# A hybrid decoder layer on 8 cores: x and y transposed, k, v and q begun while x arrives, GLU, attention and a 4-shift-packed convolution in one phase, output projection in halves

## The chip, the cores and the metric

One Trainium2 chip, 8 of its cores, each running the same program on its own share of the data. The metric is the device time of one execution in microseconds (us), taken on the slowest core. Engines: PE is TensorE (matmuls), PEld its weight loads, DVE is VectorE, ACT is ScalarE, POOL is GpSimd, SP issues DMAs.

## The reference: what is computed

One layer with two parallel groups behind one input projection, for a prompt (4 sequences of 2048) and for 32 single decode rows; model width 2048.

```python
h = rms_norm(x, norm_mix_g)
z = h @ w_in                      # columns: q 1024 | k 256 | v 256 | u_val 1024 | u_gate 1024
q = rope(rms_norm(q, q_norm_g), pos); k = rope(rms_norm(k, k_norm_g), pos)
a = attn(q, k, v, sinks)          # 16 heads of 64, 4 kv heads, window 128, a sink logit per head
u = u_val * sigmoid(u_gate)       # GLU
c = causal_dwconv(u, 31 taps); c = silu(layer_norm(c))
x = x + concat(a, c) @ w_out
x = x + square(relu(rms_norm(x, norm_mlp_g) @ w_up)) @ w_down   # 2048 -> 8192 -> 2048
```

Outputs are y, the new k, v and convolution states of the prompt, and those of the decode rows.

## The kernel before

Each core has 1024 prompt columns (half a sequence), the 128 rows before them (the halo, needed for keys and for the convolution) and 4 decode rows. Activations lie transposed, channels on the 128 partitions and tokens along the free axis: HT is the normed x in bf16 (16 channel tiles of 1160 columns), XT the residual in f32 (16 tiles of 1032: 1024 prompt, 4 decode, 4 padding), HM the input of the MLP. A weight tile is 128x128, and a projection is 16 matmuls over the input channels for each piece of columns.

The program is a list in the order of the Python code; a planner (`P.add`) gives every operation to its engine in that order and adds semaphore waits from the buffers read and written. So each engine works in order, and the order of the code is the order of its stream. Helpers record all operations of one kind, so these lines stand for many: L490 is every matmul, L494 every transpose on PE, L458 every activation on ScalarE, L462 every two-input operation of VectorE or GpSimd, L476 and L477 copies and casts (ScalarE, and VectorE or GpSimd), L445 every DMA except those of wq (L573). "arena" in the profile is the one SBUF buffer that everything lies in, "psum" the eight PSUM banks.

The stages, one after another:

1. **x** (to 64.0 us). SP loads ten row tiles of x; ScalarE makes the sums of squares (L546), VectorE scales (L551), and PE transposes each tile twice: in f32 for XT (304 transposes in all) and in bf16 for HT. GpSimd makes the rope tables, issues wkv (4 DMAs), and then wq (16) when the last x tile is in.
2. **k/v** (to 102.4) and **q** (to 168.2). Ten tiles of k/v, then nine of q, each followed by `qk_chain`, which takes norm and rope from PSUM on ScalarE, VectorE and GpSimd. `fin_qk` transposes the result.
3. **GLU** (to 288.6). For 8 channel chunks a gate and a value projection, each over three banks (`acc3`, two slots of three banks in turn, pieces of 356 columns), a sigmoid and a product. VectorE runs the 31 taps of convolution chunks 0 and 1 as multiply-adds (`conv_tap`, L718) beside it.
4. **Convolution** of chunks 2 to 7 on PE (288.6 to about 370): 31 matmuls with a diagonal matrix for each of three pieces; GpSimd builds the diagonals (multiplies of 3968 columns). Then the LayerNorm sums by matmul, until 386.6.
5. **Attention** (386.6 to 456.2). 16 units (block of 128 queries, pair of kv heads), `unit_a` and `unit_b`: 4 score matmuls and 4 that add the mask, 4 exponentials of 512 columns, 8 matmuls for output and denominator with 64 output partitions each, then 1/x as Ln and Exp. GpSimd normalizes the convolution (`ln_chunk_a`, L841) beside it. Decode attention follows, to 469.7.
6. **Output projection** (469.7 to 607.7): 16 chunks of 48 matmuls over AT (attention) and CT (convolution). After each, VectorE adds the residual, and `norm2_stats` squares the chunk before (one in four on VectorE) and adds it up by two matmuls of 512 columns.
7. **MLP** (to 1557.8): 16 groups of four hidden tiles. `up_group` is issued one group ahead of `down_group`. In the last group `out_chunk` transposes each y chunk back in f32 (nine transposes on PE, three copies on ScalarE) and stores it.

## Time and profile before

| | us |
|---|---|
| median of 6 runs (1560.15 to 1561.43) | 1560.88 |
| the profiled execution, its own time | 1559.33 |
| its span on core 5, the slowest (others from 1551.2) | 1557.8 |
| PE busy in it, matmuls and transposes | 1457.0 (94%) |
| DVE, ACT, POOL busy | 725.6, 294.1, 260.9 |
| DMA moved | 113.83 MB, 73 GB/s in the mean |
| PE's share of the chain that ended last | 87% |

The span is cut out of one execution on one core. Busy times overlap, since engines work beside each other. In a row of the timeline the first number is when it starts and the second how long it lasts, then engine, line, operation, output<-input, how many instructions it holds, and in brackets how long the engine was idle before and what ended that. In a row of the table by lines and form there stand count, busy time, mean ns of one, and idle time before. Matmuls are pipelined, so the mean of one can be longer than the step from one to the next.

### The profile page before, as it was taken

To read this page: it belongs to the slowest core of one execution; us is meant where nothing else is said; L and a number is where in the kernel's file an instruction comes from. 1 tells how busy PE (TensorE), PEld (TensorE's weight loads), DVE (VectorE), ACT (ScalarE), POOL (GpSimd) and SP (SyncE) were. 2 spreads that over 40 slices of the span, in tenths; PEclk is the share of its full clock that TensorE was granted. 3 is DMA by queue.
4 is the path that set the end of the run, shared out by engine and by line. 5 is a ranking of instruction groups with operands and counts; after the bars stand their busy time and mean duration, and the time that the engine had idled before them with its cause. 6 is when DMAs were issued, how large, how long until landed. Compare 5 with 4: busy or idle time off the path is not lost.

```text
span 1557.8 us, 23496 instructions; the slowest of 8 cores (1551.2 to 1557.8 us)
## 1 busy us (share of the span) xinstructions
PE 1457.0 (94%) x9650; PEld 926.0 (59%) x9650; DVE 725.6 (47%) x686; ACT 294.1 (19%) x456; POOL 260.9 (17%) x276
## 2 busy tenths in 40 slices
PE   3799999998979899999999999999999999999997
PEld 3444566664226556666666666666666666666665
DVE  5534268895233211263454454364355345355353
ACT  5633200102773212101001000000100100100113
POOL 2346302353920000101001000000100100100000
PEclk9999999999889999999999999999999999999999
DMA  9830244002005342746146246245335435425315
GB/s 235 181 61 36 41 76 74 17 2 15 1 10 86 56 75 47 122 82 106 31 82 108 38 73 109 47 68 103 56 67 95 67 56 95 75 54 89 68 58 161
DMA packets 63009, 113.83 MB, mean 73 GB/s; under 512 B 18882, under 2 KB 38658, under 8 KB 61724
## 3 DMA queue, kind: packets, MB, share of 16 engines
q0 software_dynamic: 43744, 90.77, 35.6%
q1 hardware_dynamic: 19160, 21.56, 4.4%
q8 instruction: 78, 1.28, 0.3%
q14 instruction: 27, 0.22, 0.1%
HBM read 194.12 MB, written 10.35 MB: 131 GB/s over the span
## 4 chain that ended last, share of the span: by engine, by line
PE 87%; DVE 4%; ACT 3%; issue 3%; DMA 3%; ACTq 0%; DVEq 0%; SPq 0%; POOL 0%; POOLq 0%
PE psum L490 85%; DVE arena L462 3%; PE psum L494 2%; ACT arena L458 1%; ACT arena L476 1%; DMA arena<-wup 1%; DMA arena<-xm 1%; DVE arena L477 1%; DMA arena<-wo 0%; DMA arena<-tab 0%; DVE arena L551 0%; ACT arena L546 0%; ACTq L255 0%; DVEq L255 0%; SPq L445 0%
## 5 line engine op out<-in xcount | busy, mean ns | idle before, releaser
L490 PE MATMUL psum<-arena 128*128 128x344 bf16 (+5 forms) x9086 | 1405.5, 317 | 49.5 <-DVE arena L462 30.5
L490 PEld LDWEIGHTS psum<-arena 128*128 128x128 bf16 (+3 forms) x9086 | 875.2, 98 | 568.2 <-issue 113.2
L462 DVE TENSOR_TENSOR arena<-psum,arena 128x1032 f32<-128x1032 f32 (+10 forms) x400 | 418.5, 1064 | 359.9 <-PE psum L490 268.0
L462 DVE TENSOR_TENSOR arena<-arena 128x1032 bf16<-128x1032 bf16 (+3 forms) x144 | 141.8, 987 | 375.2 <-ACT arena L458 368.2
L458 ACT ACTIVATE arena<-psum 128x1032 bf16<-128x1032 f32 (+8 forms) x160 | 128.0, 803 | 928.8 <-PE psum L490 904.4
L445 POOL DMA_DIRECT2D arena<-wup x64 | 33.9, 531 | 804.6 <-PE psum L490 804.6
L462 POOL TENSOR_TENSOR arena<-arena 128x256 f32<-128x256 f32 (+6 forms) x64 | 138.8, 2171 | 141.1 <-PE psum L490 63.6
L718 DVE SCALAR_TENSOR_TENSOR arena<-arena 128x1032 f32<-128x1032 bf16 (+1 forms) x90 | 123.3, 1370 | 9.4 <-DVE arena L718 0.5
L458 ACT ACTIVATE arena<-arena 128x1032 bf16<-128x1032 f32 (+10 forms) x139 | 80.7, 590 | 133.5 <-DVE arena L462 98.9
L494 PE MATMUL psum<-arena 128*128 128x128 f32 (+6 forms) x564 | 61.5, 255 | 47.3 <-DVE arena L551 27.8
L494 PEld LDWEIGHTS psum<-arena 128*128 128x128 f32 (+6 forms) x564 | 52.1, 125 | 59.3 <-issue 54.5
L476 ACT COPY arena<-psum 128x512 f32<-128x512 f32 (+9 forms) x115 | 54.3, 514 | 84.3 <-PE psum L494 74.9
L483 DVE TENSOR_REDUCE arena<-arena 128x4 f32<-128x256 bf16 (+4 forms) x20 | 16.3, 817 | 64.9 <-ACT arena L458 64.8
L445 POOL DMA_DIRECT2D arena<-wdn x64 | 34.0, 551 | 2.8 <-issue 2.6
L445 POOL DMA_DIRECT2D arena<-wo x16 | 8.6, 540 | 129.7 <-PE psum L490 129.7
L445 POOL DMA_DIRECT2D arena<-wu x16 | 8.7, 543 | 74.7 <-PE psum L490 74.7
L458 ACT ACTIVATE arena<-psum,arena 128x1032 f32<-128x1032 f32 (+2 forms) x7 | 6.8, 978 | 73.3 <-PE psum L490 73.3
L546 ACT ACTIVATE arena<-arena 128x2048 bf16<-128x2048 f32 (+1 forms) x10 | 19.2, 1922 | 6.5 <-DVE arena L487 5.3
L573 POOL DMA_DIRECT2D arena<-wq x16 | 10.6, 701 | 34.6 <-DMA arena<-xs 34.6
L551 DVE TENSOR_SCALAR arena<-arena 128x2048 bf16<-128x2048 f32 (+1 forms) x10 | 12.8, 1281 | 4.7 <-ACT arena L458 4.4
L477 DVE CAST arena<-arena 128x1032 bf16<-128x1032 f32 (+1 forms) x12 | 11.8, 1027 | 0.8 <-PE psum L490 0.7
L841 POOL TENSOR_SCALAR arena<-arena 128x1032 f32<-128x1032 f32 x8 | 9.6, 1201 | 1.4 <-POOL arena L462 1.4
(17 smaller groups left out, 35.8 us busy)
## 6 DMA issues: line engine op xcount, KB each, us to landing
arena<-wup POOLq DMA_DIRECT2D x64, 512.0 KB, 6.9
arena<-wdn POOLq DMA_DIRECT2D x64, 512.0 KB, 14.1
arena<-xm SPq DMA_DIRECT2D x8, 1024.0 KB, 10.3
arena<-wu POOLq DMA_DIRECT2D x16, 512.0 KB, 6.2
arena<-wo POOLq DMA_DIRECT2D x16, 512.0 KB, 6.2
yp<-arena SPq DMA_DIRECT2D x16, 512.0 KB, 3.2
arena<-wq POOLq DMA_DIRECT2D x16, 256.0 KB, 14.4
arena<-wkv POOLq DMA_DIRECT2D x4, 512.0 KB, 20.4
```

The costliest lines, as they stand in the source:

```text
L445: return P.add(eng, lambda e: e.dma_start(out=out.ap, in_=in_.ap), reads=[in_], writes=[out], key=key, group=group, final=final)
L458: return P.add("act", lambda e: e.activation(out=out.ap, in_=in_.ap, func=func, bias=b, scale=s), reads=rd, writes=[out])
L462: return P.add(eng, lambda e: e.tensor_tensor(out=out.ap, in0=in0.ap, in1=in1.ap, op=op), reads=[in0, in1], writes=[out])
L476: return P.add("act", lambda e: e.copy(out=out.ap, in_=in_.ap), reads=[in_], writes=[out])
L477: return P.add(eng, lambda e: e.tensor_copy(out=out.ap, in_=in_.ap), reads=[in_], writes=[out])
L483: return P.add("dve", lambda e: e.tensor_reduce(out=out.ap, in_=in_.ap, axis=AX.X, op=ALU.add), reads=[in_], writes=[out])
L490: return P.add("pe", lambda e: e.matmul(out.ap, lhsT.ap, rhs.ap, start=start, stop=stop), reads=[lhsT, rhs], writes=[out])
L494: return P.add("pe", lambda e: e.transpose(out.ap, in_.ap, ident.ap), reads=[in_, ident], writes=[out])
L546: P.add("act", (lambda xn=xn, xin=xin, ms=ms, pp=pp: (lambda e: e.activation(out=xn(p=pp).ap, in_=xin(p=pp).ap, func=AF.Square, accum_out= ...
L551: P.add("dve", (lambda xn=xn, xin=xin, rs=rs, pp=pp: (lambda e: e.tensor_scalar(out=xn(p=pp).ap, in0=xin(p=pp).ap, scalar1=rs.ap, scalar2= ...
L573: P.add("pool", (lambda kc=kc: (lambda e: e.dma_start(out=WQ(kc).ap, in_=wq_d[kc])))(), writes=[WQ(kc)], key="wq", group=True, after=xin_d ...
L718: P.add("dve", (lambda c=c, uu=uu, cc=cc, j=j: (lambda e: e.scalar_tensor_tensor(out=cc.ap, in0=uu.ap, scalar=CW(c).ap[:, j:j + 1], in1=cc.ap,
```

## The change

Nearly all of the program's first half is written anew (1468 lines of diff); the MLP's matmuls and loads stay. What it does:

- **Start.** The host hands x over transposed; 16 channel tiles of 1160 columns arrive through SP. As each lands, VectorE scales it by the norm's gain into HT, ScalarE squares it, GpSimd adds the squares, and PE multiplies three (later more) k/v tiles by it. The row scale is applied after the projections. GpSimd issues a wkv tile between the sums and wq after the last. K's `qk_chain` reads the projection from an SBUF copy (RAW). q follows in nine tiles.
- **One phase for GLU, attention and convolution.** For a channel chunk there are six `u_job` (3 pieces of 352, 352 and 356 columns, gate and value) on two PSUM banks, 6 and 7. The sigmoid is made of Exp, Ln, Exp on ScalarE, with a product on VectorE before and one on GpSimd after. Between the jobs stand two attention units a chunk, and from the third chunk on two `conv_job`. The mask is a product on VectorE in place of a matmul; decode attention (`sample_a`, `sample_b`) stands in chunk 4.
- **Convolution in 32-partition strips.** `u_done` copies u by 16 DMAs from SBUF to SBUF into U4, in four shifts and four groups of 32 channels. A matmul then takes four taps at once for 32 channels; a `conv_job` is 8 steps of 4 such strips, 512 columns wide, in all 512 matmuls. VectorE makes no taps. `conv_sums` adds up for LayerNorm on GpSimd.
- **Output projection.** First the AT half for all 16 chunks (`wo_half(dc, 0, AT)`), beside it the LayerNorm; then the CT half with the residual and `norm2`. x is loaded a second time for the residual. Squares are added on GpSimd (14 of 16), not by matmuls.
- **MLP.** Three wup tiles are loaded ahead, not two. The last down group stores XT as it is, transposed; the host turns it back.

```diff
-        for h8 in range(2):
-            pt = ps_bf16(nbank(), (8, 128))
-            for j in range(8):
-                c = 8 * h8 + j
-                tr(pt(j, (0, nt)), xn((c * 128, c * 128 + 128), p=pp), IDB((0, nt), p=(0, nt)))
-            tt("dve", HT((8 * h8, 8 * h8 + 8), (c0, c0 + nt)), pt((0, 8), (0, nt)),
-               bc(PAR((8 * h8, 8 * h8 + 8)), 2, (128, 8, nt)), ALU.mult)
+    for kc in range(16):
+        xs_ = XST[kc % 4]
+        xd.append(dma("sp", xs_(), R(xt_d[kc]), "xst%d" % (kc % 4)))
+        dma("pool", WKV(kc), R(wkv_d[kc]), "wkv%d" % kc, after=[xd[kc - 3]] if kc >= 3 else [])
+        if kc == 5:
+            dma("sp", PAR(), R(par_d), "par")
+            dma("sp", CST(), R(cst_d), "cst")
+        if kc == 8:
+            dma("sp", TABIN(), R(tab_d.rearrange("p (a b c) -> p a b c", a=2, b=10)), "tab")
+        ts("dve", HT(kc), xs_(), G1(kc), ALU.mult)
+        if kc == 0:
+            act(SS1(), xs_(), AF.Square)
+        else:
+            act(SQX[kc % 2](), xs_(), AF.Square)
+        if kc >= 2:
+            tt("pool", SS1(), SS1(), SQX[(kc - 1) % 2](), ALU.add)
+        for ti in range(NKV1):
+            tn, c0, nt = TT[ti]
+            mm(kvp[ti](p=(0, nt)), HT(kc, (c0, c0 + nt)), WKV(kc), kc == 0, kc == 15)
+    tt("pool", SS1(), SS1(), SQX[1](), ALU.add)
+    for kc in range(16):
+        dma("pool", WQ(kc), R(wq_d[kc]), "wq%d" % kc, after=[xd[15]] if kc >= 2 else [xd[13]])
...
-        qk_chain(acck, 4, nt, GCK, GSK, ti, kb_, kout(p=pp), out_f32=kf4)
+        qk_chain(RAW[ti], 4, nt, GCK, GSK, ti, kb_, K2[ti](p=pp), out_f32=kf)
...
+    for kc in range(16):
+        for i in range(3):
+            q_mm(1 + i, i, kc)
+    fin_k([0, 1, 2, 3], 6)
+    fin_k([4, 5, 6, 7], 7)
+    fin_k([8, 9], 6)
+    pend = [q_chain(1, 0), q_chain(2, 1)]
+    for i, ti in enumerate(range(4, 10)):
+        for kc in range(16):
+            q_mm(ti, i % 3, kc)
+        if i == 0:
+            pend.append(q_chain(3, 2))
+        fin_q(*pend.pop(0))
+        pend.append(q_chain(ti, i % 3))
...
-            if j == 0:
-                act(SG(), accb((0, 3), (0, UW)), AF.Sigmoid)
-                if dve_taps:
-                    conv_tap(*dve_taps.pop(0))
+    def u_job(c, pi, w, gate):
+        a, b = PU[pi]
+        n = b - a
+        acc = dense_bank(n)
+        for kc in range(16):
+            mm(acc(), w(kc), HT(kc, (U0 + a, U0 + b)), kc == 0, kc == 15)
+        flush()
+        i = gts[0] % 2
+        if gate:
+            gt, sg = GT[i]((0, n)), SGR[i]((0, n))
+            rb = RB((a, b))
+            tt("dve", gt, acc(), rb, ALU.mult)
+            act(gt, gt, AF.Exp, scale=-1.0)
+            act(gt, gt, AF.Ln, bias=1.0)
+            act(gt, gt, AF.Exp, scale=-1.0)
+            tt("pool", sg, gt, rb, ALU.mult)
+        else:
+            sg = SGR[i]((0, n))
+            tt("dve", UB[c % 2]((a, b)), acc(), sg, ALU.mult)
+            if pi == 2:
+                tt("dve", UF(c), acc((322, 356)), SGR[i]((322, 356)), ALU.mult)
+            gts[0] += 1
...
+    def u_done(c):
+        ub, u4 = UB[c % 2], U4[c % 2]
+        first = None
+        for s in range(4):
+            for g in range(4):
+                src = Ref(ub.ap[32 * g:32 * g + 32, 2 + s:2 + s + UL], ub((0, NU)).rngs)
+                dst = Ref(u4.ap[32 * s:32 * s + 32, g, 0:UL])
+                i = 4 * s + g
+                P.add("sp", (lambda src=src, dst=dst: (lambda e: e.dma_start(out=dst.ap, in_=src.ap)))(),
+                      reads=[src], writes=[u4()] if i == 0 else [], claim=[u4()] if i == 15 else [],
+                      key="u4%d" % (c % 2))
...
-        for pi, (a, b) in enumerate(PM):
-            a0 = 172 if (c == 2 and pi == 0) else a
-            n_ = b - a0
-            for j in range(31):
-                g0 = MC0 + a0 + j - 30
-                mm(accb(pi, (0, n_)), dg(j), U(c, (g0, g0 + n_)), j == 0, j == 30)
+    def conv_job(c, pi):
+        acc = dense_bank(512)
+        for t in range(8):
+            for g in range(4):
+                mm(acc(p=(32 * g, 32 * g + 32)), D4[c % 2](g, t),
+                   U4[c % 2](g, (4 * t + 512 * pi, 4 * t + 512 * pi + 512)), t == 0, t == 7)
+        flush()
+        act(CC(c, (512 * pi, 512 * pi + 512)), acc(), AF.Identity, bias=CB(c))
+    def conv_sums(c, eng="pool"):
+        act(SQT(), CC(c), AF.Square)
+        if c == 0:
+            cp(eng, S1(), CC(c))
+            cp(eng, S2(), SQT())
+        else:
+            tt(eng, S1(), S1(), CC(c), ALU.add)
+            tt(eng, S2(), S2(), SQT(), ALU.add)
...
-                mm(pss(), IDB(), bc(mb(), 1, (128, 4, 128)), False, True)
+                act(pt(), ps_f32(2 * kb + gi, 1, (4, 128))(), AF.Exp, scale=0.125)
+                tt("dve", pt(), pt(), bc(mb(), 1, (128, 4, 128)), ALU.mult)
...
+    for c in range(8):
+        wg, wv = wu.pop(0), wu.pop(0)
+        for pi in range(3):
+            for gate in (True, False):
+                u_job(c, pi, wg if gate else wv, gate)
+                if c == 0 and pi == 0 and gate:
+                    while pend:
+                        fin_q(*pend.pop(0))
+                if job % 3 == 1 and nu < 16:
+                    if nu >= 1:
+                        unit_b(nu - 1)
+                    unit_a(nu)
+                    nu += 1
+                if c == 4 and pi == 0 and not gate:
+                    sample_a()
+                if c == 4 and pi == 1 and not gate:
+                    sample_b()
+                job += 1
+            if c >= 2 and pi < 2:
+                conv_job(c - 2, pi)
+                if pi == 1:
+                    conv_sums(c - 2)
+        u_done(c)
...
-        if dc >= 1:
-            norm2_stats(dc - 1)
-            act(HM(dc - 1), XT(dc - 1), AF.Identity, scale=G2(dc - 1))
+    conv_job(6, 0)
+    conv_job(6, 1)
+    conv_sums(6, "dve")
+    unit_b(15)
+    conv_job(7, 0)
+    conv_job(7, 1)
+    conv_sums(7, "dve")
+    xt_load(7)
+    xt_load(8)
+    wo_half(0, 0, AT)
+    wo_half(1, 0, AT)
+    wo_half(2, 0, AT)
+    ln_stats()
+    for dc in range(3, 16):
+        wo_half(dc, 0, AT)
+        if dc - 3 < 8:
+            ln_chunk(dc - 3)
+    def norm2(dc):
+        sq = SQ2[dc % 2]
+        act(HM(dc), XT(dc), AF.Identity, scale=G2(dc))
+        act(sq(), XT(dc), AF.Square)
+        if dc == 0:
+            cp("pool", SS(), sq())
+        else:
+            tt("pool" if dc < 14 else "dve", SS(), SS(), sq(), ALU.add)
+    for dc in range(16):
+        wo_half(dc, 1, CT)
+        norm2(dc)
+    upq = [wstream(wup_d[i], "wup", 128) for i in range(3)]
...
-            if last and dc >= 1:
-                out_chunk(dc - 1)
+            if last:
+                dma("sp", R(yt[128 * dc:128 * dc + 128, :]), XT(dc, (0, NO)), "yt%d" % dc, final=True)
```

In the order of each engine's stream, at three places:

On PE, the end of the GLU, the convolution and the start of attention before (356 columns is a GLU piece, 34x128, 128x120 and the pieces of 172 and 344 are state, decode and prompt convolution with LayerNorm sums, 512 columns attention):

```order
L490 MATMUL psum<-arena 128x356 x720
L494 MATMUL psum<-arena 34x128 x8
L490 MATMUL psum<-arena 128x172 x31
L490 MATMUL psum<-arena 128x344 x62
L494 MATMUL psum<-arena 128x120 x8
L490 MATMUL psum<-arena 128x344 x513
L490 MATMUL psum<-arena 128x512 x8
L490 MATMUL psum<-arena 64x512 x8
```

and one channel chunk of the new phase (352 and 356 columns is GLU, 64x512 and 128x512 attention, 32x512 the convolution's strips):

```order
L483 MATMUL psum<-arena 128x356 x16
L483 MATMUL psum<-arena 128x352 x32
L483 MATMUL psum<-arena 64x512 x8
L483 MATMUL psum<-arena 128x512 x4
L483 MATMUL psum<-arena 32x512 x32
L483 MATMUL psum<-arena 128x352 x32
L483 MATMUL psum<-arena 32x512 x32
L483 MATMUL psum<-arena 128x356 x16
L483 MATMUL psum<-arena 64x512 x8
L483 MATMUL psum<-arena 128x512 x4
```

GLU, convolution and attention were three blocks; now no more than 32 matmuls of one kind stand in a row.

On POOL, the start before (640 columns are the rope tables, 256 the K chains):

```order
L462 TENSOR_TENSOR arena<-arena 128x640 x4
L487 MEMSET arena 128x16x4
L487 MEMSET arena 128x256
L487 MEMSET arena 128x16x4 x2
L445 DMA arena<-wkv 128x4x512 x4
L573 DMA arena<-wq 128x1024 x16
L462 TENSOR_TENSOR arena<-arena 128x256 x2
L477 CAST arena<-arena 128x256
```

and now, from the last of the sums of squares (1160 columns) on:

```order
L437 DMA arena<-wkv 128x512
L454 TENSOR_TENSOR arena<-arena 128x1160 x2
L437 DMA arena<-wq 128x1024 x16
L473 CAST arena<-arena 128x128 x4
L473 CAST arena<-arena 128x32
L454 TENSOR_TENSOR arena<-arena 128x640 x4
L480 MEMSET arena 128x8x4
L454 TENSOR_TENSOR arena<-arena 128x256 x2
L473 CAST arena<-arena 128x256
```

The wq issues stand behind fifteen sums of squares, and the tables and the five casts between them and the first K chain.

On PE, the last down group before (each y chunk's transposes behind the next chunk's 12 matmuls):

```order
L490 MATMUL psum<-arena 128x344 x5976
L494 MATMUL psum<-arena 128x128 x8
L494 MATMUL psum<-arena 4x128
L490 MATMUL psum<-arena 128x344 x12
L494 MATMUL psum<-arena 128x128 x8
L494 MATMUL psum<-arena 4x128
```

and now, from the last GLU job to the end:

```order
L483 MATMUL psum<-arena 128x356 x16
L483 MATMUL psum<-arena 32x512 x64
L483 MATMUL psum<-arena 64x512 x8
L483 MATMUL psum<-arena 32x512 x64
L483 MATMUL psum<-arena 128x344 x6921
```

Output projection and MLP are now one run of 6921 matmuls of 344 columns, with no statistics and no transposes among them; four conv jobs and half an attention unit stand before it.

## Rows read from the trace of the kernel before

**Rows 1.** The page: the span, and TensorE's granted clock in 40 slices, in tenths.

```profile
span 1557.8 us, 23496 instructions; the slowest of 8 cores (1551.2 to 1557.8 us)
...
PEclk9999999999889999999999999999999999999999
```

**Rows 2.** Table by stage, core 5 (columns as told above).

```profile
0.00:64.00 64.00, 29.04 (x304) 27.39 (x304) 40.27 (x35) 41.53 (x78) 20.51 (x32) 0.96 0.89 217
386.60:456.20 69.60, 67.76 (x256) 18.77 (x256) 19.43 (x30) 57.83 (x97) 44.92 (x24) 0.90 0.00 1
456.20:469.70 13.50, 2.03 (x57) 1.76 (x57) 4.93 (x8) 7.96 (x13) 1.74 (x3) 0.59 0.34 55
469.70:607.70 138.00, 127.75 (x822) 81.31 (x823) 31.60 (x26) 37.07 (x36) 8.46 (x16) 0.95 0.40 68
668.60:1502.20 833.60, 817.80 (x5592) 544.72 (x5591) 404.35 (x355) 58.78 (x57) 58.25 (x110) 1.00 0.43 73
```

**Rows 3.** Timeline of PE: output projection, second up group, an MLP group, last down group.

```profile
510.07 31.48 PE L490 MATMUL psum<-arena 128*128 128x512 bf16 x200 [2.62 <-DVE arena L462]
...
652.76 16.42 PE L490 MATMUL psum<-arena 128*128 128x344 bf16 x100 [3.10 <-DMA arena<-wup]
...
1359.75 56.20 PE L490 MATMUL psum<-arena 128*128 128x344 bf16 x384 [1.05 <-DVE arena L462]
...
1503.76 1.91 PE L490 MATMUL psum<-arena 128*128 128x344 bf16 x12
...
1507.04 1.91 PE L490 MATMUL psum<-arena 128*128 128x344 bf16 x12
```

**Rows 4.** Table by lines and form, 386.6 to 456.2 us (attention).

```profile
L458 ACT ACTIVATE arena<-psum 128x512 bf16<-128x512 f32 x64 | 37.9, 597 | 9.5 <-PE psum L490 7.7
L462 POOL TENSOR_TENSOR arena<-arena 128x1032 f32<-128x1032 f32 x15 | 35.5, 2366 | 5.6 <-ACT arena L458 4.6
...
L458 ACT ACTIVATE arena<-arena 128x512 f32<-128x512 f32 x30 | 18.8, 626 | 1.4
L462 DVE TENSOR_TENSOR arena<-psum,arena 128x512 f32<-128x512 f32 x15 | 10.2, 682 | 6.8 <-PE psum L490 6.8
```

**Rows 5.** The page: costliest groups, and DMA issues (KB each, us to landing).

```profile
L573 POOL DMA_DIRECT2D arena<-wq x16 | 10.6, 701 | 34.6 <-DMA arena<-xs 34.6
L551 DVE TENSOR_SCALAR arena<-arena 128x2048 bf16<-128x2048 f32 (+1 forms) x10 | 12.8, 1281 | 4.7 <-ACT arena L458 4.4
...
arena<-wup POOLq DMA_DIRECT2D x64, 512.0 KB, 6.9
...
yp<-arena SPq DMA_DIRECT2D x16, 512.0 KB, 3.2
```

**Rows 6.** Timeline of DVE at the start and in the convolution, then of POOL.

```profile
9.06 6.53 DVE L477 CAST arena<-arena 128x128 bf16<-128x128 f32 x4
...
273.88 9.67 DVE L718 SCALAR_TENSOR_TENSOR arena<-arena 128x1032 f32<-128x1032 bf16 x7
...
288.35 12.12 DVE L718 SCALAR_TENSOR_TENSOR arena<-arena 128x1032 f32<-128x1032 bf16 x3
...
282.95 15.03 POOL L462 TENSOR_TENSOR arena<-arena 128x3968 bf16<-128x3968 bf16 x2 [16.74 <-PE psum L490]
```

**Rows 7.** Table by lines and form, whole span: the K chains, a cache load.

```profile
L462 POOL TENSOR_TENSOR arena<-arena 128x256 f32<-128x256 f32 x18 | 12.0, 667 | 22.3 <-DVE arena L462 20.8 <-POOL arena L462 0.6 <-PE psum L490 0.4
...
L445 POOL DMA_DIRECT2D arena<-ck x1 | 4.6, 4620 | 0.0
L462 DVE TENSOR_TENSOR arena<-psum,arena 128x256 f32<-128x256 f32 x9 | 3.7, 415 | 0.0
```

**Rows 8.** Timeline of PE, one q tile.

```profile
145.99 7.07 PE L490 MATMUL psum<-arena 128*128 128x512 bf16 x32
```

**Rows 9.** Table by lines and form, PE, 430.85 to 431.20 us (attention, 64-column matmuls).

```profile
L490 PE MATMUL psum<-arena 128*64 128x512 bf16 x4 | 0.6, 391 | 0.0
```

**Rows 10.** Timeline of SP, four copies between partitions ahead of decode attention.

```profile
385.39 2.49 SPq L445 DMA_DIRECT2D arena<-arena  x4
```

971 lines of the change are left out of this document (417 added, 554 removed).

## The prediction, made before the changed kernel ran

> **What bounds the kernel now.** I read the page first [rows 1]: in a span of 1557.8 us TensorE has its full 2.4 GHz in all but two of 40 slices, so clock is not the matter as a whole. The table by stage [rows 2] says how dense TensorE is where; time can only go where it does work that can be left out, or waits. The MLP from 668.6 to 1502.2 us is dense: 384 matmuls of 344 columns take 56.2 us [rows 3], 146 ns each, in a period of 57.2. Four other places are loose. From 0 to 64 TensorE is busy 29 us, and only with transposes of x. From 288.6 to 386.6 it makes a convolution of 31 taps, and then waits for LayerNorm. From 386.6 to 456.2 (attention) it shows as busy, but ScalarE holds 57.8 of the 69.6 us and a unit's matmuls wait for its exponentials; from 456.2 to 469.7 nearly everything waits. And in the last down group 12 matmuls (1.75 us) are followed by nine f32 transposes and a wait, a pitch of 3.3 us [rows 3].
>
> The profiled execution took 1559.33 us by its own time, 1.5 over its span; the median of the runs is 1560.88. I make the sum in span and add 3.1 at the end.
>
> **Step 1, start to the first GLU matmul: 168.2 us to about 157.** Removed are the 304 transposes of x and their evacuations. In their place x arrives transposed in 16 tiles, and GpSimd adds each tile's squares: 15 adds of 1160 columns, 2.37 us x 1160/1032 = 2.66 each [rows 4]. Between them it issues the wkv loads (0.66 each, as for wq [rows 5]). The row to watch is another: seven multiply-adds on VectorE take 9.7 us while GpSimd is idle, but three take 12.1 us across two GpSimd multiplies that take 15.0 together, and at the start four small casts take 6.5 us beside GpSimd's products [rows 6]. VectorE stands still while a GpSimd instruction runs, if both inputs of its own are in SBUF, or for a plain cast. The scaling of x is of the cast's kind and takes 0.7 us (1.28 for 2048 columns [rows 5], here 1160). So a tile costs 2.66 + 0.66 = 3.3 if nothing excludes, 4.0 if the scaling alternates with all of it; I take 3.7, since it can fall into an issue. First add near 9 us, so the last ends near 64 (58 to 72). x is 9.5 MB, 44 us at the 217 GB/s of now [rows 2], so GpSimd ends last. Only then come, in its order, 16 wq issues (10.6 us [rows 5]), five casts and four table products (about 8 us), and then ten K chains. These now read the projection from SBUF, not PSUM, so they fall under the row above: GpSimd 0.67 twice and a cast of 0.4, VectorE 0.41 and two halves, some 0.55 [rows 7], alternate, about 2.9 us a tile, 29 in all; without exclusion 2.0. K is ready near 112 (103 to 116). TensorE has three kv tiles (10.4 us), some f32 column sums (4 us) and the first three q tiles (96 matmuls at 0.22 us, 21) to do by 101, then waits for K's transposes. Six q tiles of 7.07 us [rows 8] and 0.3 of transposes end at 157 (147 to 168). Gain 11.
>
> **Step 2, GLU, convolution, LayerNorm, both attentions: 301.5 us to about 225.** Removed are 31-tap matmuls for most of eight chunks and all VectorE taps, the mask matmuls and the LayerNorm stall. The GLU's own 768 matmuls stay (0.15 us each by columns, 115). Convolution: 512 matmuls that each write a strip of 32 partitions. No row shows a strip of 32. The nearest row is attention's 64-column matmuls: four take 0.6 us at a mean of 391 ns each [rows 9], so two start together and the next two about 0.22 us later. If four strips start together likewise, 128 groups x 0.22 to 0.24 = 28 to 31 us; if only two, 55; if none, 111. I take 31, since strips that start together is the pattern of the row.
> Per channel chunk TensorE has 6 GLU jobs (14.4 us), two attention units (6 pairs each, 2.8), two conv jobs (3.8), and half a microsecond or so of changes of shape: 21 to 22. ScalarE has nine passes over 352 columns (0.49 each, scaled from 0.63 for 512), eight exponentials at 0.60, four passes at 0.63 [rows 4], two evacuations and a square: 14. VectorE has about 11, GpSimd 9. None exceeds TensorE, but GLU and conv have two banks, 6 and 7, and a bank is free only after gate multiply (0.55), three ScalarE passes, GpSimd's multiply (0.85) and the value multiply (0.55): 4 us with the hand-offs, and one unit's 3.6 us of ScalarE stands in that line twice a chunk, ahead of it. Laying these durations out for one chunk in the order of the streams, TensorE waits 1.2 us at the second gate and 2.6 at the second value: 24.8 us a chunk, 21.4 for the first two, which have no conv. For the exclusion of rows 6 I add 1 us a chunk (0 to 9). At the loop's start TensorE waits 5 us for the last q chain, and GpSimd issues the two cache loads, one of them 4.6 us now [rows 7], ahead of the first gate's multiply: 4 more. 6 x 25.8 + 2 x 22.4 + 9 = 209. The tail: the last chunk's 16 shift copies are issued on SP at up to 0.62 us, as four copies between partitions now [rows 10], so they land 9 to 14 us after the last GLU matmul's evacuation; TensorE covers 7 of that. Tail 16. x comes back as 8.5 MB while the first projection chunks run; its first tile lands just before the first add. 209 + 16 = 225, gain 76.5.
>
> **Step 3, output projection: 138.0 to 129.** Its 768 matmuls (112.3) stay; 32 statistics matmuls (7 us) and four stops of 2.6 us on VectorE's squares [rows 3] go, since squares are now summed on GpSimd (2.4 us against 3.5 of TensorE). Added: f32 LayerNorm sums in two banks with their evacuation (5), VectorE's 3.7 us a chunk against 3.5 (2), and a new wait. The first wup loads stand on GpSimd behind the sum for chunk 13, whose end I put 1 us before the projection's, and land 6.9 us later [rows 5]: 6 plus 2 of slow clock. Without that 121.
>
> **Step 4, MLP up to the last group: 894.5 to 890.** Unchanged but for a stop in the second up group that a third wup load in flight removes: 3.1 us, and the next 100 matmuls take 16.4 [rows 3], 1.8 more than at 146 ns each; I take 4.5. **Step 5, last down group: 55.6 to 34.** 16 x 1.75 = 28.1, then one add (1.2), one issue (0.4, estimated) and 3.2 to 4.5 for the store. Stores go out at 300 GB/s; the backlog is unknown, 0 to 12 us, nearest 0 to 1 since 512 KB lands in 3.2 us now [rows 5].
>
> Sum: -11 - 76.5 - 9 - 4.5 - 21.5 = -122.5, so a span of 1435 and, at the median's 3.1 above span, 1438 us. A measurement of this kernel can tell about 0.2% from no change.
>
> **The rivals.**
> Interleaving hides everything (0.16): TensorE paces the loop, 6 x 22 + 2 x 18 = 168 in place of 209, 1397 us. For it: no engine is above 14 us of 22. Against it: two banks only, and in-order ScalarE.
> VectorE and GpSimd alternate through the loop (0.18): GpSimd reads SBUF for about 9 us a chunk (three gate products, diagonals 1.8, sums 4.7), and eight mask multiplies, now from SBUF, wait in line with the gates. All of it in the chain is 72 us, 8 are counted: 1470 to 1500. Rows 6 speak for it; that VectorE with one PSUM input is 0.68 us with GpSimd at work [rows 4] speaks against it for the gates. The Trainium skill states it as a rule (page "SBUF — State Buffer", section "Who interferes with whom"): two SBUF inputs on VectorE, or one of its two-port fast modes, exclude a GpSimd instruction that reads SBUF, and whoever starts first keeps the port to its end. The trace agrees, with three multiply-adds in 12.1 us. By that rule in full this rival is the forecast.
> The packing does not do what it says (0.10): strips run one after another, +10 us a chunk of which 3.8 falls into waits, and all of it in the tail: some 6 x 6.2 + 20 = 57, about 1495.
> Slower than before (0.03): TensorE at 1.2 GHz. From 456.2 to 469.7, with 2 us of matmuls in 13.5, it is granted 0.59 [rows 2]. Kv, q, GLU, attention and conv are some 265 us of matmuls at full clock. If all ran at half, +265 less 50 of waits they would fill, 1650; it is slower than before when half speed holds for 60% of them. Against it: the loop is planned 85% busy, and 67.8 of 69.6 us in attention kept 0.90.
>
> **How the numbers follow.** Forecast as summed 0.52; the remaining 0.01 is a front end so late that the gain nearly vanishes. 1438 is the forecast's centre; its own range is 1410 to 1465. 1388 takes in the first rival with an early front end, 1497 the second and part of the third. Faster 0.96, same 0.01, slower 0.03.
>
> **What would show it.** Right: the first 352-column matmul at 147 to 168 us; GLU chunks 24 to 27 us apart; four 32-column matmuls starting within 20 ns; a wup wait of about 6 us before the first up group; last matmul 5 to 6 us before the end; period of 57.2 in the MLP unchanged. Wrong: a loop at 22 us a chunk, or at 30 and more with VectorE's mask multiplies far above 0.6 us; strips one by one; stores that land long after the last add; a granted clock near 0.5 in the loop.

## The result, and the profile after

The changed kernel takes **1461.24 us** in the median, against 1561.2 of the kernel before in the same measurement: a ratio of 0.935, with a 95% interval of 0.9338 to 0.9364. That is 100 us less, 6.4%. The forecast was 1438 with a range of 1388 to 1497 and a gain of 122.5; the time lies 23 us above its centre.

One thing is needed to read the numbers: in this kernel pairs of neighbouring cores often have a stretch of some 161 us at a granted clock of 0.81 (from 114 to 276 us here, with a piece at half clock in it), and in the profiled execution cores 6 and 7 have it. Lines of the page, then of the view of the cores:

```profile
span 1459.8 us, 22456 instructions; the slowest of 8 cores (1446.6 to 1459.8 us)
...
PE 1346.1 (92%) x9007; PEld 834.3 (57%) x9016; DVE 696.1 (48%) x734; ACT 286.0 (20%) x424; POOL 312.1 (21%) x330
...
PEclk9988788899899999999999999999999999999999
```

```profile
core 0: 1451.3 us, clock 0.974
...
core 6: 1459.8 us, clock 0.956
```

So I read the stages on core 0, which has no such stretch, and count the 8.5 us to core 6 apart. These 8.5 are a net. Core 6 is 9.6 us later than core 0 at the first GLU matmul, 11.7 at the projection and 15.0 at the last down group (the 3 in the projection come on cores 1 and 5 too, without the stretch); then it gains 6.4, since on core 0 the stores end latest of all eight cores, 16.7 us behind the last matmul for 10.2 on core 6. The profiled execution took 1461.33 by its own time, 1.5 above its span. The table by stage of core 0, cut where the prediction's steps end (a row has its start and end, its length, the busy us and count of PE, of weight loads, of DVE, ACT and POOL, then TensorE's granted clock, the share of the DMA engines, and GB/s); the loop with its tail, and the last down group, answer to [rows 2, 3]:

```profile
0.00:60.70 60.70, 31.65 (x106) 11.14 (x109) 47.73 (x20) 20.01 (x17) 49.85 (x35) 0.92 0.81 214
60.70:153.65 92.95, 82.97 (x430) 39.83 (x435) 52.38 (x79) 38.52 (x91) 72.01 (x77) 0.96 0.54 93
153.65:366.90 213.25, 176.23 (x1412) 93.82 (x1416) 84.45 (x178) 101.52 (x191) 79.05 (x64) 0.94 0.44 74
366.90:391.25 24.35, 11.35 (x138) 4.49 (x137) 8.74 (x15) 5.96 (x10) 3.24 (x3) 0.72 0.79 155
391.25:513.97 122.72, 116.23 (x784) 77.00 (x781) 64.96 (x58) 49.65 (x48) 42.37 (x30) 0.99 0.56 115
513.97:1406.60 892.63, 875.16 (x5960) 582.42 (x5961) 416.67 (x368) 70.03 (x70) 65.67 (x124) 1.00 0.45 75
1406.60:1451.30 44.70, 27.97 (x192) 18.15 (x190) 20.96 (x17) 0.00 (x0) 0.00 (x0) 0.84 0.81 189
```

| step of the prediction | before | forecast | core 0 | off |
|---|---|---|---|---|
| 1: to the first GLU matmul | 168.2 | 157 | 153.65 | -3.4 |
| 2: GLU loop and tail | 301.5 | 209 + 16 | 213.25 + 24.35 | +12.6 |
| 3: output projection | 138.0 | 129 | 122.7 | -6.3 |
| 4: MLP to the last group | 894.5 | 890 | 892.6 | +2.6 |
| 5: last down group | 55.6 | 34 | 44.7 | +10.7 |
| the slowest core's low clock | | 0 | 8.5 | +8.5 |

The sum of the last column, 24.7 (24.8 unrounded), is what the span of 1459.8 has over the forecast's 1435. Step 3 ends where the first up group starts, at 513.97.

The last two channel chunks and the tail on core 0, in the timeline of PE and then of SP:

```profile
345.78 8.40 PE L483 MATMUL psum<-arena 128*128 128x352 bf16 x76 [2.10 <-DVE arena L454]
355.78 12.97 PE L483 MATMUL psum<-arena 128*128 128x352 bf16 x124 [1.59 <-ACT arena L450]
371.29 4.53 PE L483 MATMUL psum<-arena 128*32 128x512 bf16 x40 [2.54 <-DVE arena L454]
386.28 13.89 PE L483 MATMUL psum<-arena 128*32 128x512 bf16 x124 [10.46 <-DMA arena<-arena]
```

```profile
371.17 11.80 SPq L776 DMA_DIRECT2D arena<-arena  x16
...
1409.80 26.58 SPq L437 DMA_DIRECT2D yt<-arena  x16
```

Each chunk has a wait of about 2 us for VectorE and one of 1.6 for ScalarE; the tail one of 10.5 for the copies. The chunks' last GLU matmuls lie 25.2, 25.6, 32.9, 25.9, 25.6 and 25.6 us apart from the third chunk on; 25.8 was forecast, and the 32.9 has decode attention in it.

### The profile page after: what moved, and what is told of

Read it like the earlier page. It is cut to its first block, busy times and chain, and to the rows that moved or that the text cites. A ratio compares the mean times of both kernels' runs of the same rounds, so it can differ in the third digit from the quotient of the medians.

```text
span 1459.8 us, 22456 instructions; the slowest of 8 cores (1446.6 to 1459.8 us)
## 1 busy us (share of the span) xinstructions
PE 1346.1 (92%) x9007; PEld 834.3 (57%) x9016; DVE 696.1 (48%) x734; ACT 286.0 (20%) x424; POOL 312.1 (21%) x330
## 4 chain that ended last, share of the span: by engine, by line
PE 83%; DVE 6%; issue 3%; ACT 3%; DMA 2%; POOL 1%; SPq 1%; DVEq 0%; ACTq 0%; POOLq 0%
PE psum L483 82%; DVE arena L454 4%; ACT arena L450 2%; DVE arena L467 2%; DMA arena<-xt 1%; POOL arena L454 1%; SPq L776 1%; DMA arena<-wup 0%; ACT arena L472 0%; DMA arena<-arena 0%; DVE arena L476 0%; PE psum L487 0%; SPq L437 0%; DVEq L265 0%; DVE arena L473 0%
## 5 line engine op out<-in xcount | busy, mean ns | idle before, releaser
L483 PE MATMUL psum<-arena 128*128 128x344 bf16 (+7 forms) x8915 | 1340.3, 327 | 93.3 <-DVE arena L454 32.0
L483 PEld LDWEIGHTS psum<-arena 128*128 128x128 bf16 (+4 forms) x8924 | 828.0, 100 | 601.6 <-issue 183.6
L454 DVE TENSOR_TENSOR arena<-psum,arena 128x1032 f32<-128x1032 f32 (+7 forms) x408 | 423.0, 1049 | 305.2 <-PE psum L483 275.7
L454 DVE TENSOR_TENSOR arena<-arena 128x1032 bf16<-128x1032 bf16 (+6 forms) x252 | 205.3, 826 | 423.6 <-ACT arena L450 407.3
L450 ACT ACTIVATE arena<-psum 128x512 bf16<-128x512 f32 (+6 forms) x150 | 112.5, 787 | 808.8 <-PE psum L483 793.5
L454 POOL TENSOR_TENSOR arena<-arena 128x1032 f32<-128x1032 f32 (+8 forms) x112 | 190.9, 1715 | 186.0 <-ACT arena L450 148.8
L450 ACT ACTIVATE arena<-arena 128x352 f32<-128x352 f32 (+11 forms) x237 | 148.9, 647 | 221.5 <-DVE arena L454 136.8
L467 DVE TENSOR_SCALAR arena<-arena 128x1160 bf16<-128x1160 f32 (+2 forms) x25 | 50.2, 2045 | 12.4 <-DMA arena<-xt 11.2
L437 POOL DMA_DIRECT2D arena<-wdn x64 | 34.0, 551 | 27.9 <-PE psum L483 25.8
L472 ACT COPY arena<-psum 128x1024 bf16<-128x1024 bf16 (+5 forms) x18 | 13.0, 764 | 22.8 <-PE psum L483 12.7
L437 POOL DMA_DIRECT2D arena<-wkv x16 | 12.3, 769 | 0.9 <-POOLq L297 0.9
L450 ACT ACT_TABLE_LOAD x3 | 3.8, 1283 | 23.3 <-PE psum L483 11.4
```

The costliest lines, as they stand in the source:

```text
L437: return P.add(eng, lambda e: e.dma_start(out=out.ap, in_=in_.ap), reads=[in_], writes=[out], key=key, group=group, final=final, after=after)
L450: return P.add("act", lambda e: e.activation(out=out.ap, in_=in_.ap, func=func, bias=b, scale=s), reads=rd, writes=[out])
L454: return P.add(eng, lambda e: e.tensor_tensor(out=out.ap, in0=in0.ap, in1=in1.ap, op=op), reads=[in0, in1], writes=[out])
L467: return P.add(eng, lambda e: e.tensor_scalar(out=out.ap, in0=in0.ap, scalar1=a, scalar2=b, op0=op0, **kw), reads=rd, writes=[out])
L472: return P.add("act", lambda e: e.copy(out=out.ap, in_=in_.ap), reads=[in_], writes=[out])
L483: return P.add("pe", lambda e: e.matmul(out.ap, lhsT.ap, rhs.ap, start=start, stop=stop), reads=[lhsT, rhs], writes=[out])
```

## The experiments

Spans and pitches below are of cores without the low-clock stretch where nothing else is said; the changed kernel's spans are 1446.6 to 1452.5 us (cores 0 to 5), in the mean 1450.3. All but the last three versions ran one to three times, so these are cores of one profiled execution, and a difference of 2 us is no more than a hint. The pitch is the time from the last GLU matmul of one channel chunk to that of the next; chunks are numbered from 0, as in the code.

**Strips one after another (e1_strips).**

```diff
-        for t in range(8):
-            for g in range(4):
+        for g in range(4):
+            for t in range(8):
```

> The 32 matmuls of a conv job run strip by strip (8 steps of one 32-partition strip, then the next) instead of the four strips in turn. Theory: four strips run beside each other only because neighbours in the stream write different strips; a job of 1.91 us (0.24 us for four) becomes 32 x 0.22 = 7.0 us, 10 us a chunk more, of which up to 4 fall into waits that are there: the chunk pitch of 25.6 us rises to 32 to 36, the whole by 45 to 80 us. Rival: strips never ran beside each other, or the order does not matter: the job stays at 1.9 us and the time within 3 us.

A conv job took 4.54 us instead of 1.91, the chunk pitch was 30.7 instead of 25.6 in most of the late chunks, and spans were 1473.4 to 1485.1 (six cores), some 30 us more. One job in the changed kernel (core 0), then one of this run (core 1), lines by form:

```profile
L483 PE MATMUL psum<-arena 128*32 128x512 bf16 x32 | 1.9, 380 | 0.0
```

```profile
L483 PE MATMUL psum<-arena 128*32 128x512 bf16 x32 | 4.5, 380 | 0.0
```

In the changed kernel four strips run beside each other (their starts lie 3 to 4 ns apart, the next four 205 ns later). So the order of the stream matters and the packing works; but one after another costs 2.4 times, not the 3.7 of the expectation. The starts of a job tell why: four matmuls alone, 216 ns apart, then twelve pairs, then four alone. The rows do not name the strip, but this is what comes out if the first four matmuls of a strip run beside the last four of the strip before, and the matmuls of one strip never beside each other. Neither theory had that price.

**No mask product (e8_nomask)**, and **the gate's last product on VectorE (e7_gate).**

```diff
-                tt("dve", pt(), pt(), bc(mb(), 1, (128, 4, 128)), ALU.mult)
```

> Leaves out the mask product of attention (64 products on VectorE, 0.43 us each); all else as in the changed kernel. Theory (VectorE's order): the gate and value products that free the two PSUM banks stand behind the masks, which wait for ScalarE's exponentials; without them the waits of 1.5 us behind a unit go and the chunk pitch falls from 25.6 to about 23 us, the whole by 15 to 22 us. Rival (ScalarE's order): the banks wait for the gate's three ScalarE passes behind the unit's exponentials; then the pitch falls by under 1 us a chunk, the whole by 0 to 7 us.

```diff
-            tt("pool", sg, gt, rb, ALU.mult)
+            tt("dve", sg, gt, rb, ALU.mult)
```

> The gate's last product runs on VectorE instead of GpSimd (24 products of about 0.93 us become about 0.43). Theory (length of the chain from gate to value): each piece's value product can start 0.5 us earlier, where it is waited for, at 2 of 3 pieces: the pitch falls by 0.5 to 1.0 us, the whole by 4 to 8 us. Rival (VectorE and GpSimd shut each other out): the products also stop blocking the masks, and the pitch falls by 2 us or more, the whole by 15 us or more. Second rival: the product on VectorE delays the next bank as much: within 2 us of no change.

Without masks the pitch was 22.7 to 23.1 us in the last three chunks and spans 1426.0 to 1435.4, about 18 less: the first theory. The waits in the timeline of PE, for two chunks (core 0):

```profile
311.10 21.58 PE L483 MATMUL psum<-arena 128*128 128x352 bf16 x184 [1.54 <-ACT arena L450]
334.07 11.28 PE L483 MATMUL psum<-arena 128*128 128x352 bf16 x96 [1.40 <-ACT arena L450]
```

The wait for VectorE is gone, the one for ScalarE is left. With the gate's product on VectorE the pitch of the last three chunks rose to 26.0 to 26.8 (25.6 to 25.9 before), and spans were 1447.7 to 1456.2, some 2 us more: the second rival. Rows of masks in the changed kernel's loop, then with the gate on VectorE (lines by form, core 0):

```profile
L454 DVE TENSOR_TENSOR arena<-arena 128x512 bf16<-128x512 bf16 x60 | 32.0, 559 | 33.8 <-ACT arena L450 32.3
```

```profile
L454 DVE TENSOR_TENSOR arena<-arena 128x512 bf16<-128x512 bf16 x60 | 26.6, 447 | 31.8 <-ACT arena L450 29.2
```

A mask takes 0.43 us where nothing is in its way. So VectorE and GpSimd do shut each other out in the loop, for 60 x 0.11 = 7 us at the masks, but taking the gate's product off GpSimd gives less than it puts into VectorE's line, and the time is not less. The rival by which exclusion sets the loop is out. That the masks' place in VectorE's order sets it, and not their work, the next run tests.

**Masks later (e9_defer).** A unit's masks go into a list, and the next GLU job empties it behind its own product.

```diff
-                tt("dve", pt(), pt(), bc(mb(), 1, (128, 4, 128)), ALU.mult)
+                masks.append((pt, mb))
...
             gts[0] += 1
+        run_masks()
```

> All mask products stay, but each unit's four stand on VectorE behind the next GLU job's gate or value product instead of ahead of it. Theory (VectorE's order, not its work, holds the PSUM banks): nearly all that leaving the masks out gave comes back without leaving anything out, a chunk pitch of 23 to 24 us instead of 25.6 and the whole 10 to 18 us less. Rival (it is the work of the masks, 3.4 us of VectorE a chunk): the pitch stays over 25 us, the whole within 4 us.

On the die without the stretch (cores 4 to 7) the pitch was 24.2 to 24.3 us in most of the last three chunks (25.9 in the others), and spans 1435.1 to 1441.1, some 12 less than the changed kernel's, towards the low end of the theory. With the masks' work unchanged, their order alone gives about 1.4 of the 2.6 us a chunk that leaving them out gave. The rest shows as a wait of 2.0 for ScalarE (core 5):

```profile
318.70 19.09 PE L483 MATMUL psum<-arena 128*128 128x352 bf16 x168 [2.02 <-ACT arena L450]
```

Chunk 1 fell from 23.3 to 18.2 us, and chunk 2 took 26.5 to 32.7 instead of 25.2: on three of the four cores its first conv job now waited 3.3 to 8.2 us for the shift copies of chunk 0. These stand on SP behind four small copies that wait for a load of the decode cache, which landed at 190 to 193 us, some 28 us after its issue. In the changed kernel it lands as late (192.7), but there the loop is late enough to hide it.

**Decode's key copy earlier (e6_decode).**

```diff
     def sample_a():
-        ktn = KT((0, 2), (SC0, SC0 + SPC))
-        cp("dve", Ref(KTS.ap[:, :, :, 127], KTS().rngs), Ref(ktn.ap.rearrange("p c s -> p s c"), ktn.rngs))
...
+        if c == 2:
+            ktn = KT((0, 2), (SC0, SC0 + SPC))
+            cp("dve", Ref(KTS.ap[:, :, :, 127], KTS().rngs), Ref(ktn.ap.rearrange("p c s -> p s c"), ktn.rngs))
         u_done(c)
```

> The one small copy of the decode keys on VectorE (0.19 us) stands at the end of channel chunk 2 instead of right before decode attention in chunk 4. Theory: TensorE's wait of 6.25 us in chunk 4 is this copy standing in VectorE's order behind the unit's masks; it goes, and with it the slow first conv job behind it (3.6 us instead of 1.9): chunk 4 from 32.9 to 25 to 27 us, the whole 5 to 8 us less. Rival: the wait is the unit's own exponentials and masks, which come late anyway: chunk 4 keeps over 31 us.

Chunk 4 took 30.3 to 30.9 us instead of 32.9, and spans were 1444.4 to 1451.2 (cores 0 to 3): about 2 us less, between the two. The timeline of PE in chunk 4, before this edit (core 0) and with it (core 1):

```profile
271.27 20.91 PE L483 MATMUL psum<-arena 64*128 64x4 bf16 x204 [6.25 <-DVE arena L473]
```

```profile
269.06 0.16 PE L483 MATMUL psum<-arena 64*128 64x4 bf16 x1 [3.83 <-ACT arena L450]
```

The copy held 2.4 us. The rest is ScalarE: `sample_a` writes its scores to banks 0 and 1 right behind a unit whose exponentials still read them. Placed one value job later, behind no unit (in the joint version), that wait was 0.67.

**Sums of squares on VectorE (e2_sums_dve).**

```diff
-            tt("pool", SS1(), SS1(), SQX[(kc - 1) % 2](), ALU.add)
+            tt("dve", SS1(), SS1(), SQX[(kc - 1) % 2](), ALU.add)
```

> The sums of squares while x arrives run on VectorE instead of GpSimd. Theory (GpSimd paces the start, and VectorE's scaling only fits into its DMA issues): a tile costs VectorE about 0.8 + 1.3 = 2.1 us instead of GpSimd's 3.42; then x's own arrival is the limit, 9.5 MB at about 217 GB/s, 44 us: the last k/v matmul of the first phase ends near 52 to 55 us instead of 61, and the first GLU matmul comes 5 to 9 us earlier than 153.65. Rival (x's arrival or its four buffers paced it already): within 2 us of before.

The last scaling of x ended at 53.0 us, not 60.1 (core 0), but the first GLU matmul came at 150.2 and 151.5 (cores 0 and 1), 3.4 and 1.7 us earlier than on the same cores of the changed kernel: half of what was expected, or less. Their spans were 1441.5 and 1447.7, 9.8 and 4.8 less, so part of that gain came from elsewhere. The rows of scaling and sums of the changed kernel, then of this one (lines by form, core 0, the x phase):

```profile
L467 DVE TENSOR_SCALAR arena<-arena 128x1160 bf16<-128x1160 f32 x16 | 47.3, 3013 | 11.2 <-DMA arena<-xt 11.2
L454 POOL TENSOR_TENSOR arena<-arena 128x1160 f32<-128x1160 f32 x15 | 40.0, 2668 | 9.5 <-ACT arena L450 9.1
```

```profile
L454 DVE TENSOR_TENSOR arena<-arena 128x1160 f32<-128x1160 f32 x15 | 20.4, 1360 | 0.1
...
L467 DVE TENSOR_SCALAR arena<-arena 128x1160 bf16<-128x1160 f32 x16 | 13.2, 824 | 21.7 <-DMA arena<-xt 21.6
```

A scaling takes 0.82 us when GpSimd rests and 3.01 when it adds: it stands until the add is over, and gets its turn while GpSimd issues a DMA. Then x's arrival is the limit. GpSimd came to the K chains 10.9 us earlier for it (68.0 for 78.9), but there stood 6.5 us for ScalarE, which makes the gate's row scale ahead of them and itself waits for TensorE's last k/v tile; the chains ended 5.0 earlier (96.7 for 101.7). Another 2 us went behind TensorE's halt there, where the first q tile took 10.0 us, not 8.1, longer at half clock.

**Last two down groups in one (e3_merge)**, **copies on two queues (e4_copies)**, **wup earlier (e5_wup).**

```diff
+    parts = [(HID[g % 2], wdq[g], fi) for g in (NG - 2, NG - 1) for fi in range(GFF)]
+    for dc in range(16):
+        for n, (hid, wd, fi) in enumerate(parts):
+            for pi, (a, b) in enumerate(PM):
+                mm(accb(pi, (0, PW)), wd[fi](dc), hid(fi, (a, b)), n == 0, n == 2 * GFF - 1)
```

> The last two down groups become one: for each of the 16 output chunks 24 matmuls (3.5 us) and one add, then its store, instead of 12 matmuls (1.75 us) twice. Theory (the stores are the bound at the end): 16 stores of 528 KB take about 2.3 us each, more than the 1.75 us in which chunks come, so 15 us are left behind the last add; at 3.5 us a chunk each store ends before the next, and the time behind the last add falls to 3 to 6 us: the whole 9 to 12 us less. Rival (the last store has a latency of its own, or the stores are issued late): the tail stays over 12 us and the time within 3 us.

```diff
+        two = c == 7
...
+                if two:
+                    mine = [u4((0, 2)) if g < 2 else u4((2, 4))]
+                    P.add("sp" if g < 2 else "pool",
```

> For the last channel chunk the 16 shift copies are issued half by SP and half by GpSimd, which is idle there. Theory (the issues of 0.59 us one after another on SP hold the last conv jobs): TensorE's wait of 10.46 us before the last chunk's conv jobs falls by 8 x 0.59 = 4.7 us, to 5 to 7 us; the whole 3 to 5 us less. Rival (the copies compete for the DMA engines with the reload of x and the weights): the wait stays over 9 us.

```diff
         norm2(dc)
+        if dc in (9, 11, 13):
+            upq.append(wstream(wup_d[len(upq)], "wup", 128))
```

> The first three wup loads are issued in the second half of the output projection, behind the sums of chunks 9, 11 and 13, instead of all behind the sum of chunk 13. Theory: the wait of 4.3 us before the first up group and the slow clock behind it (52 matmuls in 10.7 us, 7.6 at full clock) go: 4 to 8 us less. Rival (the sums and the statistics behind them hold the start): the wait is replaced by another of the same size, within 2 us.

*Stores.* From the last matmul to the end it was 5.3 to 6.6 us on the eight cores, instead of 10.2 to 16.7, and the spans of cores 4 and 5 were 1442.1 and 1437.7: the theory. The page's DMA issues of the changed kernel, then the same of this one in its last 60 us (core 5); before, a store landed in 3.2 [rows 5]:

```profile
yt<-arena SPq DMA_DIRECT2D x16, 514.0 KB, 8.2
```

```profile
yt<-arena SPq DMA_DIRECT2D x16, 514.0 KB, 3.9
```

*Copies.* TensorE's wait before the last conv jobs fell from 8.5 to 10.8 on the eight cores to 4.6 to 4.8: the theory. The time did not follow everywhere, because the projection, now earlier, caught up with the reload of x (timeline of PE, core 0):

```profile
382.45 17.52 PE L483 MATMUL psum<-arena 128*32 128x512 bf16 x140 [4.78 <-DMA arena<-arena]
...
431.26 9.01 PE L483 MATMUL psum<-arena 128*128 128x344 bf16 x50 [3.52 <-DVE arena L454]
```

The 3.5 us are an add that waits for its x tile. Six cores had such a wait, of 1.5 to 5.2; spans without the stretch were 1443.7 to 1453.6, in the mean 1.6 less.

*wup.* All eight cores had the stretch in this run, so I take the time from the projection's first matmul to the last of all: 1036.6 to 1039.5 us, against 1043.2 to 1047.0 in the changed kernel, 7 less: the theory. The changed kernel's wait (core 7), which is gone from the same view here:

```profile
523.02 11.19 PE L483 MATMUL psum<-arena 128*128 128x344 bf16 x52 [4.21 <-DMA arena<-wup]
```

**All of it together (e10_all).** Besides the edits above: the row scale behind the K chains, the last q transposes two pieces later, the cache loads behind the first chunk, x tiles 0 to 3 reloaded during the loop, LayerNorm's and the norm's sums by pieces.

```diff
-    ln_stats()
+    ln_stats([0])
     for dc in range(3, 16):
         wo_half(dc, 0, AT)
+        if dc < 5:
+            ln_stats([dc - 2])
...
+        if 3 <= c < 7:
+            xt_load(c - 3)
```

> Together: masks behind the next product; sums of squares on VectorE at the start, and the gate's row scale worked out behind the K chains; decode attention one job after its unit instead of right behind it, its key copy early; the last q transposes and the cache loads later in the first chunk; the last chunk's copies on two queues, and four tiles of x reloaded during the loop; LayerNorm and norm sums one piece at a time between the projection's chunks; wup early; the last two down groups as one. Theory (each wait is its own, and none stands behind another of the same size): 8 for the start, 5 at the loop's start, 12 in the loop, 5 for decode, 6 for the copies, 3 for LayerNorm, 5 for wup, 8 for the stores: about 50 us less than the changed kernel, 1405 to 1420 us. Rival (the waits cover each other, or TensorE's slow clock takes them back): less than half, over 1435 us.

1415.5 us, ratio 0.908 to the kernel before (0.9047 to 0.9112), 46 less than the changed kernel: the theory. But chunk 2 (the second in the text of the next expectation) took 38 to 43 us. Its place in the timelines of PE and POOL and the DMA issues of 150 to 225 us (core 4):

```profile
206.11 8.64 PE L483 MATMUL psum<-arena 128*128 128x352 bf16 x44 [12.54 <-DMA arena<-wu]
```

```profile
170.37 4.59 POOL L437 DMA_DIRECT2D arena<-cv  x1
174.96 1.94 POOL L454 TENSOR_TENSOR arena<-arena 128x1024 bf16<-128x1024 bf16 x1
176.82 1.14 POOL L437 DMA_DIRECT2D arena<-wu  x2
```

```profile
arena<-wu POOLq DMA_DIRECT2D x4, 512.0 KB, 23.6
...
arena<-cv POOLq DMA_DIRECT2D x1, 254.0 KB, 31.9
```

A load of 254 KB took 31.9 us, and the weights issued behind it 23.6; in the changed kernel, in the same stretch of the program, the load took 30.4 and the weights 11.3. TensorE's wait for the weights was 8.5 to 12.5 us on the eight cores. The edit that hid the cache loads from one place had put them ahead of the weights of the next.

**The cache loads moved, and more (e11_more).** The loads go into the loop over the q tiles, behind the first weights of the GLU; in a conv job ScalarE and VectorE share the evacuation.

```diff
+        if i == 2:
...
+            dma("pool", KTS((0, SPC), (0, 2), (0, 127)), R(ckt), "cks", group=True)
+            dma("pool", CVB(p=(0, 127)), R(cv[:, 1:128, :].rearrange("s k d -> k s d")), "cks", group=True)
...
+        if pi == 0:
+            ts("dve", CC(c, (0, 512)), acc(), CB(c), ALU.add)
```

> All of the joint version before, and: the cache loads issued in the q phase instead of ahead of the weights of channel chunk 2; the casts and K's tables on GpSimd while x arrives, the first q chain ahead of the K transposes; the first conv job of a chunk evacuated by VectorE instead of ScalarE. Theory (the new wait of 12.5 us in the second chunk is its weights, queued behind a cache load of some 9,000 small packets): the second chunk falls from 38 to 43 us to about 24, 13 us or more; 4 to 8 us more from the start, and up to 1.5 us a chunk from the evacuation: 1385 to 1400 us. Rival (the weights are late by themselves, their slots come free too late): the second chunk stays over 33 us, and the whole over 1405.

Chunk 2 fell to 23.5 us and the later ones to 22.7 to 23.6, as the theory has it. From the start nothing came (first GLU matmul at 149.6 to 155.7 us, 150.1 to 152.6 in the version before, where 4 to 8 less were expected), and the median was 1405.8 (ratio 0.9005, 0.8993 to 0.9017), not under 1400. The view of the cores says why:

```profile
core 2: 1383.9 us, clock 0.992
core 3: 1383.3 us, clock 0.990
core 4: 1402.8 us, clock 0.971
core 5: 1404.2 us, clock 0.972
```

In each of its five runs at least one pair of neighbours had the stretch, and it costs 20 us now. Chunks 1 to 3 lie in it: on cores with it they take 9 us more than on cores without, in the changed kernel 1 us more, where waits took it in. Table by stage of core 5 with it, then of core 2 without:

```profile
104.00:163.00 59.00, 57.75 (x265) 26.28 (x264) 26.68 (x32) 18.46 (x31) 38.40 (x21) 0.83 0.47 46
163.00:268.00 105.00, 102.60 (x685) 52.38 (x684) 40.76 (x99) 52.37 (x100) 33.91 (x32) 0.80 0.53 100
268.00:330.00 62.00, 59.62 (x538) 32.60 (x537) 28.86 (x64) 33.94 (x65) 30.03 (x23) 0.99 0.56 108
```

```profile
163.00:268.00 105.00, 97.55 (x819) 53.63 (x818) 47.35 (x113) 55.95 (x107) 39.09 (x35) 0.98 0.57 113
```

**TensorE's wait before the stretch filled (e12_fill).**

```diff
     for kc in range(16):
-        for i in range(3):
+        for i in range(2):
             q_mm(1 + i, i, kc)
...
+    k_tile(8)
+    k_tile(9)
+    for kc in range(16):
+        q_mm(3, 2, kc)
     fin_k([4, 5, 6, 7], 7)
-    fin_k([8, 9], 6)
...
         if i == 0:
+            fin_k([8, 9], 6)
```

> The last version with one change of order: K's last two chains, the third q tile and the K transposes are placed so that TensorE goes on with matmuls from 92 to 100 us, where it now waits 7.1 us. Theory (the stretch of 0.81 granted clock, from about 113 to 268 us on pairs of cores, follows TensorE's wait and restart there): with the wait gone no pair has it, the slowest core is near 1380, the time 1376 to 1390 us, the mean granted clock of every core over 0.985. Rival (the stretch follows the dense matmuls as such, or chance, not the wait): some pairs still have it, from much the same time on, and the time stays between 1395 and 1406 us.

This run settles nothing. The wait of 7.1 us became five of 0.6 to 4.3, spread over 91 to 122 us, so it was not taken away; one run of seven had no pair with the stretch and took 1391.7, the others 1407.5 and more; the ratio is 0.9007 (0.8964 to 0.905). On core 0 the stretch now lay from 129 to 291 us (granted 1.00 from 124 to 128.5, 0.81 from 129 to 291, 1.00 from 296 on), some 21 us later than in the version before (108 to 269) at both ends; the last halt before it, at half clock, was later too (to 124 for 104). That speaks for the theory, and that most runs still have it speaks for the rival. The best version measured is the one before, 1405.8 us, 55 less than the changed kernel.

## Why the prediction was right, and where it was off

**What bounds the kernel** was read rightly: the four loose places gave most of the time and the output projection 15 us, the dense MLP gave 2, and its period stayed 57.2 us.

**Step 1** said 157, and 153.65 came. The reason was right too: GpSimd paces x's arrival, at 3.41 us a tile (an add of 2.64 and an issue of 0.82, which overlap a little) where 3.7 was taken; the alternation added nothing, because the scaling fits into the issue. On this the Trainium skill's rule ("SBUF — State Buffer", section "Who interferes with whom") holds as the trace shows it: a scaling of 0.82 us stands for 3.0 while GpSimd adds. For the K chains 29 us were taken and 23 came: 2.3 a tile, nearer to the forecast's 2.0 without exclusion than to its 2.9 with it. K was done some 10 us before the forecast's 112, but TensorE waited for VectorE until 106.8 and restarted at half clock, so that only 3.4 us arrived.

**Step 2** is where the largest miss lies, 12.6 us. The loop's terms held: 25.6 a chunk for 25.8, a conv job of 1.91 as if four strips start together (13 of 16; the others, at half clock, 2.9 to 3.6), 1 us a chunk for exclusion where the masks show 0.9. What failed is "209" as a sum over chunks that are alike: decode attention has no term in it, though its stage is in the 301.5, and its price in chunk 4 was 7.3 us (32.9 for 25.6). Of TensorE's wait of 6.25 there the run with the earlier copy showed 2.4 to be VectorE's order, and in the joint version, where decode stands behind no unit, 0.67 is left, which points to ScalarE's banks for nearly all the rest. Chunk 0 with the loop's start took 28.8 for 31.4, so the loop as a whole is over by 4 (213.2 for 209); the other 8 are the tail's. **The tail** was said to be 16 and was 24.35: an issue was priced rightly (13 of 16 at 0.59 us, then 3.7 to land). But the first came 4.5 us after the last GLU matmul, since the last value product stands on VectorE behind four masks; the copies landed 15 us later, for 9 to 14; and unit and conv jobs were done 10.5 us before that, so they covered 4.6 and not 7, at a mean granted clock of 0.72 over the tail.

**Step 3** had the new wait right in place and roughly in size (4.3 us for 6; 4.2 to 6.2 over the eight cores), and the matmuls (112.1 for 112.3). The LayerNorm sums took 6.3 for 5 (twelve f32 matmuls with two waits for ScalarE). It was off by the VectorE adds, whose "2" for 3.7 us against 3.5 were never on the path; by the 2 of slow clock, which fell behind the cut, into step 4; and by 1.7 that it never had: the terms given, 112.3, 5, 2, 6 and 2, add up to 127.3, not to 129.

**Step 4** is 2.6 over by that slow clock: behind the wait for the first wup load the first up group ran at half clock (52 matmuls in 10.7 us, 7.6 at 146 ns each; timeline of PE, core 0):

```profile
513.97 10.70 PE L483 MATMUL psum<-arena 128*128 128x344 bf16 x52 [4.26 <-DMA arena<-wup]
```

The third wup load landed at 520.5, long before its turn, and the stop in the second up group is gone, as forecast.

**Step 5** failed at "nearest 0 to 1": the backlog of the stores, between 0 and 12 us, was taken from a landing time of 3.2 us [rows 5] that held at a pitch of 3.3 us. The transposes that were taken away had been spacing the stores. At a pitch of 1.75 us sixteen stores of 514 KB keep the DMA engines 81% busy over the whole 44.7 us (core 0), at 189 GB/s, and 10 to 17 us are left behind the last matmul. The merged down groups bring the pitch to 3.5 us, and the tail to 5.3 to 6.6. On core 6, the slowest, the last group took 38.4 us, 4.4 over the forecast; what makes that core late stands before it.

**The rivals.** That interleaving hides everything is out (25.6 a chunk, not 22), though the later versions come to 22.7 to 23.6. That VectorE and GpSimd alternate through the loop is out by the masks' rows and by the gate's run. The packing does what it says, by the run with the strips in turn. TensorE was at 1.2 GHz only in four short stretches of the loop (160 to 171, 198 to 201, 270 to 277 and 321 to 324 us on core 0, each granted 0.50 to 0.53), at 0.94 in the mean. But the stretch at 0.81 cost the slowest core time, 8.5 us net, and no rival had it. That the time lies within the forecast's own 1410 to 1465 is in part luck: steps 1 and 3 came out 9.7 us short and took back some of the rest, and decode's price and the low clock were in no term.

## What to carry to other kernels

When work is taken out between transfers, price the transfers anew at the new pitch: a landing time holds only at the spacing at which it was read. In an in-order engine look at what stands ahead of the operation that frees a bank, for moving four small products back in the line gave 12 of the 18 us that leaving them out gave. And when something is moved out of one line, ask into which it goes: a load of 254 KB put ahead of the weights took back 8.5 to 12.5 us.
